# Turning the softmax blocks on VectorE and placing them by a DRAM copy, in a fused attention and gMLP block

## The chip, the cores and the metric

One Trainium2 chip, one of its cores. The metric is the device time of one execution in microseconds (us). All arrays are fp32; TensorE multiplies them as fp32r parts (a high part and a remainder, three products for one).

## What is computed

One layer of a hybrid decoder trunk over 1,024 tokens of width 1,024. With h the RMS-normalised input, one projection `h @ w_in` gives q, k, v, the gates and the inputs of the gMLP branch. The part that the change touches is the sliding-window attention: 16 query heads of width 64, 2 key/value heads, a window of 128 keys, a shared bias and one sink per head:

```
scores = q @ k.T * HEAD_DIM**-0.5 + bias        # a block of 128 queries against 256 keys, masked to the window
m      = max(max(scores), sink)
p      = exp(scores - m)
probs  = p / (sum(p) + exp(sink - m))
out    = probs @ v
y_a    = (out * silu(gate_a)) @ w_branch_a
merged = sigmoid(mg_a) * y_a + sigmoid(mg_b) * y_b
x      = x + rms_norm(merged @ w_out)
```

## The kernel before, in words

After a first stage (norm, v-branch, keys and values) come 24 column pairs n = 0 to 23 of the projection. A pair is made of seven products of twelve 128x512 matmuls each (a fast matrix scheme with seven products in the place of eight), so it has seven steps s = 0 to 6. Pairs 0 to 15 alternate: even n are "Q" pairs (query columns and their gate), odd n are "M" pairs (the two merge gates). Pairs 16 to 23 are "U" pairs (gMLP). After the pairs come three 1,024-cubed products in squares (branch A, branch B, output).

Attention is woven into the pairs. A head pair p (two heads, 0 to 7) has eight blocks of 128 queries. Its steps are counted by k: `attention_at(n, s)` gives p = (n - 1) // 2 and k = s for odd n, k = s + 7 for even n, so a head pair has fourteen steps, and attention ends inside pair 16. TensorE runs the first six matmuls of a product, then `attend(p, k)`, then the other six. In block order, for block k:

- step k: TensorE `scores` into the PSUM region `ps_s` (one buffer); VectorE merges the two key blocks by `copy_predicated` (line 2073), adds the bias, scales and takes the row's extreme (line 2076), into `neg_s`; ScalarE `exps` reads `neg_s` and writes `prob` (three buffers). GpSimd puts the sinks into `neg_s` at k = 0 (line 1788).
- step k+1: VectorE `reciprocal` (line 2057), ScalarE `norm` (line 1526).
- step k+3: TensorE `transpose_p` turns the two 128x128 blocks with the identity into `ps_p` in PSUM (line 997); VectorE makes the high part and the remainder from it into `pt_pack` (lines 2066 and 2067); GpSimd masks the copy for the previous keys into `pt_prev` (line 1796).
- step k+5: TensorE `values` (line 1017), two blocks to a group `g` in `ps_m`.
- at k = 7, 9, 11, 13: ScalarE moves a group's halves to `o_tmp` (lines 1541, 1542), VectorE adds them (lines 2086, 2087); at k = 8, 10, 12, 13 GpSimd multiplies by the gate (line 1806); SyncE stores to `ga_d` at k = 10 and 13.

Every engine walks the same list of pairs and steps in its own program order: at each step first `attend`, then `after(n, s)`, with waits on semaphores. So an engine that waits at one place holds up all behind it. In `after`, ScalarE copies TensorE's products out of PSUM and makes the high parts `w_hi` of the next weights, VectorE adds the products up (`c_11`, `c_22`, `c_21`, lines 2014, 2018, 2023), multiplies gates (line 2043) and, for U pairs, sums weights (lines 1998 to 2009) and runs the gMLP arithmetic (`u_mix` line 2100, `u_gate` line 2118), GpSimd makes the remainders `w_lo` (line 1751) and the weight sums of the pairs before 16. SyncE issues all DMAs: two 512 KB weight columns per pair into three `raw` buffers (line 499), the gates' stores, the bias tile of the next head pair at k = 8, and at pair 16, step 2, `bmat` and two mix tiles (lines 752 and 660) into `ub`, which lies over the keys, queries and bias of the attention.

## Time and the profile before

| | before |
|---|---|
| median of 3 runs | 908.63 us (907.77 to 910.6) |
| the profiled execution, its own time | 907.86 us |
| its span, first to last instruction | 906.1 us |
| TensorE busy | 898.7 us, 99% of the span |
| VectorE / ScalarE / GpSimd busy | 640.1 / 491.0 / 499.4 us |
| granted TensorE clock | 0.998 |
| DMA moved | 122.50 MB, 135 GB/s |

The span is what the trace covers; the execution's own time is 1.8 us more. TensorE overlaps successive matmuls, so that its busy time is best read as "no gaps", and the cost of a piece of its work from the distance between starts.

### The profile page before, as it was taken

The numbers are of one execution on the slowest core, as the hardware profiler recorded it, in microseconds if no ns is written. First come the engines' busy times: TensorE is split into PE (matmuls) and PEld (weight loads), VectorE is DVE, ScalarE is ACT, GpSimd is POOL, SyncE is SP. The second block draws the span as 40 slices with busy tenths as digits, with TensorE's granted clock in tenths as the row PEclk, the third lists the DMA queues.
The fourth block names the chain that finished last, engine by engine and source line by source line (L and its number), as shares of the span: only waits on it lengthen the run. The fifth ranks groups of instructions, "written<-read, shape, count | busy, mean of one in ns | idle before, by whom it ended". The sixth has DMA issues, their size and how long they took to land.

```text
span 906.1 us, 12649 instructions
## 1 busy us (share of the span) xinstructions
PE 898.7 (99%) x4332; PEld 754.0 (83%) x4332; DVE 640.1 (71%) x1135; ACT 491.0 (54%) x948; POOL 499.4 (55%) x395
## 2 busy tenths in 40 slices
PE   9999999999999999999999999999999999999997
PEld 7888888888888888888888888888888888888886
DVE  6766794655656564656565678688689878989968
ACT  6554355766756675757566664344444434534563
POOL 4565235777686868695868685445542252043236
PEclk9999999999999999999999999999999999999999
DMA  8889764422222253323222243533188550435004
GB/s 307 195 200 247 243 204 106 136 77 90 71 91 85 82 139 129 94 77 98 72 84 91 82 150 95 187 122 122 59 303 323 186 209 1 139 116 210 1 1 186
DMA packets 126591, 122.50 MB, mean 135 GB/s; under 512 B 23208, under 2 KB 95936, under 8 KB 126272
## 3 DMA queue, kind: packets, MB, share of 16 engines
q1 hardware_dynamic: 124288, 118.27, 41.2%
q10 hardware_dynamic: 2240, 3.43, 1.2%
q8 instruction: 35, 0.57, 0.3%
q14 instruction: 28, 0.23, 0.1%
HBM read 89.68 MB, written 35.15 MB: 138 GB/s over the span
## 4 chain that ended last, share of the span: by engine, by line
PE 98%; ACT 0%; DVE 0%; POOL 0%; issue 0%; DVEq 0%; POOLq 0%; ACTq 0%
PE acc L970 51%; PE acc L1150 11%; PE acc L823 9%; PE ps_m L1150 7%; PE ps_t L1150 7%; PE ps_t L987 3%; PE ps_m L1017 3%; PE acc L913 2%; PE ps_t L997 2%; PE ps_t L853 1%; PE ps_m L853 0%; PE acc L1042 0%; PE ps_t L839 0%; PE ps_t L855 0%; PE ps_m L855 0%
## 5 line engine op out<-in xcount | busy, mean ns | idle before, releaser
L970 PE MATMUL acc<-mv,w_hi 128*128 128x512 f32 x1344 | 353.1, 392 | 0.0
L970 PEld LDWEIGHTS acc<-mv,w_hi 128*128 128x128 f32 x1344 | 245.0, 188 | 45.0
L970 PE MATMUL acc<-mv,w_lo 128*128 128x512 f32 x672 | 181.1, 391 | 0.0
L970 PEld LDWEIGHTS acc<-mv,w_lo 128*128 128x128 f32 x672 | 126.2, 188 | 28.3
L1751 POOL TENSOR_TENSOR w_lo<-sums,w_hi 128x1024 fp32r<-128x1024 f32 x48 | 116.0, 2418 | 46.4 <-ACT w_hi L1316 38.4
L1751 POOL TENSOR_TENSOR w_lo<-raw,w_hi 128x1024 fp32r<-128x1024 f32 (+1 forms) x48 | 95.7, 1994 | 41.5 <-ACT w_hi L1309 35.9
L1150 PE MATMUL acc<-right,left 128*128 128x512 f32 x432 | 98.7, 389 | 0.0
L1150 PEld LDWEIGHTS acc<-right,left 128*128 128x128 f32 x432 | 81.0, 188 | 17.2 <-DVE left L2131 0.4
L1796 POOL TENSOR_SCALAR_AFFINE_SELECT pt_prev<-pt_pack 128x512 fp32r<-128x512 f32 x64 | 41.7, 652 | 85.7 <-DVE pt_pack L2067 85.7
L1518 ACT ACTIVATE prob<-neg_s,neg_max 128x129 f32<-128x129 f32 x128 | 50.6, 397 | 68.6 <-DVE neg_max L2076 68.5
L823 PE MATMUL acc<-mv 128*128 128x512 f32 x288 | 69.3, 394 | 0.6 <-ACT mv L1183 0.6
L1150 PE MATMUL ps_t<-right,left 128*128 128x512 f32 x288 | 67.2, 389 | 0.0
L1150 PE MATMUL ps_m<-right,left 128*128 128x512 f32 x288 | 67.2, 389 | 0.0
L1150 PEld LDWEIGHTS ps_m<-right,left 128*128 128x128 f32 x288 | 54.1, 188 | 11.2
L1150 PEld LDWEIGHTS ps_t<-right,left 128*128 128x128 f32 x288 | 54.1, 188 | 11.2
L823 PEld LDWEIGHTS acc<-mv 128*128 128x128 f32 x288 | 53.2, 188 | 12.1 <-ACT mv L1183 0.8
L2086 DVE TENSOR_TENSOR o_tmp<-ps_m,o_tmp 64x256 f32<-64x256 f32 x32 | 13.3, 417 | 63.6 <-ACT o_tmp L1542 62.9
L1526 ACT ACTIVATE prob<-prob,inv_den 128x128 f32<-128x128 f32 x128 | 43.9, 391 | 8.8 <-DVE inv_den L2057 8.8
L1368 ACT ACTIVATE c<-acc 128x512 f32<-128x512 f32 x24 | 14.4, 600 | 56.1 <-PE acc L970 46.2
L2066 DVE CAST pt_pack<-ps_t 128x256 fp32r<-128x256 f32 x64 | 26.8, 419 | 24.4 <-PE ps_t L997 24.1
L2076 DVE CUSTOM_DVE_ANT_0 neg_s<-ps_t,bias_t,sink_b 128x128 f32<-128x128 f32 x128 | 39.9, 349 | 2.0
L1757 POOL TENSOR_TENSOR left<-w_a,left 128x1024 fp32r<-128x1024 f32 x7 | 18.6, 2683 | 36.6 <-ACT left L1457 36.6
(282 smaller groups left out, 1680.8 us busy)
## 6 DMA issues: line engine op xcount, KB each, us to landing
raw<-in_w_in SPq DMA_DIRECT2D x56, 512.0 KB, 4.0
ht_d<-sums SPq DMA_DIRECT2D x8, 512.0 KB, 5.1
mix_d<-mix_b SPq DMA_DIRECT2D x8, 512.0 KB, 3.9
ga_d<-gate SPq DMA_DIRECT2D x16, 256.0 KB, 2.0
tb<-tb_d SPq DMA_DIRECT2D x4, 1024.0 KB, 5.2
ub<-mix_d SPq DMA_DIRECT2D x7, 512.0 KB, 3.5
gb_d<-ub SPq DMA_DIRECT2D x7, 512.0 KB, 2.6
x_both<-in_x SPq DMA_DIRECT2D x6, 512.0 KB, 6.3
```

What stands on the lines that cost most here:

```text
L823: ins = nc.tensor.matmul(acc[b][:, hf * HALF:(hf + 1) * HALF], left, right, start=(m < 2), stop=(m >= 46), skip_group_check=True)
L970: ins = nc.tensor.matmul(bank, (w_lo if y == 2 else w_hi)[:, left + k * P:left + (k + 1) * P], right[:, (OPW if y == 1 else 0) + k * HALF: ...
L987: ins = nc.tensor.matmul(ps_s[:, h * 256 + lo:(h + 1) * 256], q_st[h][:, blk * P:(blk + 1) * P], kbuf[:, kc + lo:kc + 256], start=a, stop= ...
L1017: ins = nc.tensor.matmul(o, v_st[:, v0:v0 + P], pt[blk % 2][:, y * 256:(y + 1) * 256].rearrange("p (h c) -> p h c", h=2), start=(kb == 0 a ...
L1150: ins = nc.tensor.matmul(bank, l[:, c:c + P], r[:, (OPW if y == 1 else 0) + k * HALF:(OPW if y == 1 else 0) + (k + 1) * HALF], start=(m == ...
L1518: ins = nc.scalar.activation(prob[blk % 3][:, h * SINK_W:(h + 1) * SINK_W], neg_w(blk, h), ACT.Exp, scale=-1.0, bias=neg_max[:, head(blk, ...
L1526: ins = nc.scalar.activation(w, w, ACT.Copy, scale=inv_den[:, head(blk, h)])
L1751: nc.gpsimd.tensor_tensor(w_lo[:, c], src, w_hi[:, c].bitcast(f32), ALU.subtract).then_inc(wlo_ok, 1)
L1757: ins = nc.gpsimd.tensor_tensor(left[f % 2][:, OPW:2 * OPW][:, c], left_src(f // 7, ORDER[f % 7])[:, c], left[f % 2][:, c].bitcast(f32), A ...
L1796: nc.gpsimd.affine_select(out=pt_prev[blk % 2][:, :].rearrange("p (y q) -> p y q", y=4), in_=pt_pack[blk % 2][:, :].rearrange("p (y q) -> ...
L2066: own.link(nc.vector.tensor_copy(pack[:, 0:256], ps_p))
L2076: ins = nc.vector.tensor_tensor_reduce(out=neg_w(k, h)[:, 0:P], in0=ps_s[:, h * 256 + P:(h + 1) * 256], in1=bias_t[:, bias:bias + P], scal ...
```

## The change

- TensorE's `transpose_p` is gone (128 transposes of 128x128), and so are `ps_p`, `neg_s` and the semaphores around them.
- VectorE writes the scaled scores straight into `prob`, which now has two buffers of two blocks each (a "double block"), and the sinks by a copy of two columns per block; ScalarE's `exps` works in place.
- After `norm`, VectorE turns each 128x128 block in place with `nc.vector.transpose`, which turns every 32x32 square where it stands. The squares are then brought to their places by DRAM: SyncE stores a double block (256 KB in rows of 512 bytes) to `prob_d` (`prob_away`, k = 2, 5, 8, 11), waits for the landing and reads it back with four DMAs of 64 KB in runs of 128 bytes into `turned_in`, one buffer (`prob_back`, k = 3, 6, 9, 12). `prob_back` also waits until VectorE has read the double block before out of `turned_in`.
- VectorE's high part and remainder are now made from `turned_in` in SBUF and no longer from PSUM.
- The eight blocks' scores go to steps 0, 1, 3, 4, 6, 7, 9, 10; high part and remainder to steps 5, 6, 8, 9, 11, 12, 14, 15; GpSimd's mask one step after, `values` two steps after these; the groups' ends to 9, 12, 15, 18 and the gate to 10, 13, 16, 19. So a head pair runs on for six steps under the next, and attention ends in pair 17.
- `o_tmp` has one buffer. The bias of the next head pair is loaded at k = 11. For pairs before 16 the weight loads move from steps 4 and 5 to steps 5 and 6. `load_k(1)` moves from pair 8 step 2 to step 4, the reload of `v_st` from pair 8 step 5 to pair 9 step 4. At pair 16, step 2, SyncE waits for `scores_used` of all 64 blocks in the place of `scores_ok`.
- Some semaphores and small tiles are shared with others to make room.

The core of the diff:

```diff
+BLOCK_AT = (0, 1, 3, 4, 6, 7, 9, 10)
+LAST_STEP = 20
+    prob_d = nc.dram_tensor("prob_d", [4 * HEAD_PAIRS, P, 4 * P], f32)
...
-                prob = [sb(f"prob{b}", [P, 2 * SINK_W], f32, s1) for b in range(3)]
-                o_tmp = [sb(f"o_tmp{b}", [P, 256], f32, s1) for b in range(2)]
+                prob = [sb(f"prob{b}", [P, 4 * SINK_W], f32, s1) for b in range(2)]
+                o_tmp = sb("o_tmp", [P, 256], f32, s1)
+                turned_in = sb("turned_in", [P, 512], f32, s1)
...
+        def attention_all(n, s):
+            k = 7 * (n - 1) + s
+            p = k // 14
+            last = [(p - 1, k % 14 + 14)] if 1 <= p <= HEAD_PAIRS and k % 14 + 14 < LAST_STEP else []
+            return last + ([(p, k % 14)] if 0 <= k and p < HEAD_PAIRS else [])
+        def blocks_at(k, lag):
+            return [i for i, t in enumerate(BLOCK_AT) if t + lag == k]
+        def low_at(k, lag):
+            return [i for i in range(8) if 3 * (i // 2) + i % 2 + lag == k]
...
+            def prob_away(j):
+                sp.wait_ge(turn_ok, 2 * j + 2)
+                sp.dma_start(prob_d[j, :, :].rearrange("p (c j) -> p c j", c=4),
+                             prob[j % 2][:, :].rearrange("p (c j) -> p c j", c=4)[:, :, 0:P]).then_inc(prob_out[j % 2], 16)
+            def prob_back(j):
+                sp.wait_ge(prob_out[j % 2], 16 * (j // 2 + 1))
+                if j:
+                    sp.wait_ge(ptl_ok, 2 * j)
+                for g in range(4):
+                    sp.dma_start(turned_in[32 * g:32 * (g + 1), :].rearrange("a (c q b) -> a c q b", c=4, q=4),
+                                 prob_d[j, :, :].rearrange("(q a) (c g b) -> g a c q b", q=4, c=4, g=4)[g]
+                                 ).then_inc(prob_in[j % 2], 16)
             def attend(p, k):
+                if k in (2, 5, 8, 11):
+                    prob_away(4 * p + k // 3)
+                if k in (3, 6, 9, 12):
+                    prob_back(4 * p + k // 3 - 1)
...
-                    if s == 4:
+                    if s == (5 if n < FIRST_U else 4):
                         load_pair(n + 2, 0)
-                    if s == 5:
+                    if s == (6 if n < FIRST_U else 5):
                         load_pair(n + 2, 1)
                     if n == FIRST_U and s == 2:
-                        sp.wait_ge(scores_ok, 8 * HEAD_PAIRS)
+                        sp.wait_ge(scores_used, 8 * HEAD_PAIRS)
                         sp.dma_start(bmat, bmat_d[:, :]).then_inc(bmat_in, 16)
...
-            def transpose_p(p, blk):
-                s = 8 * p + blk
-                pe.wait_ge(prob_ok, s + 1)
-                if s:
-                    pe.wait_ge(ptl_ok, s)
-                for h in range(2):
-                    ins = nc.tensor.transpose(ps_p[:, h * P:(h + 1) * P], prob[blk % 3][:, h * SINK_W:h * SINK_W + P],
-                                              ident[:, :])
-                ins.then_inc(pt_done, 1)
...
             def attend(p, k):
-                if 5 <= k < 13:
-                    values(p, k - 5)
-                if 3 <= k < 11:
-                    transpose_p(p, k - 3)
-                if k < 8:
-                    scores(p, k)
+                for blk in low_at(k, 7):
+                    values(p, blk)
+                for blk in blocks_at(k, 0):
+                    scores(p, blk)
...
+                for blk in low_at(k, 5):
+                    s = 8 * p + blk
+                    dve.wait_ge(prob_in[s // 2 % 2], 64 * (s // 4 + 1))
                     if s == 0:
                         dve.wait_ge(v_out, 16)
                     if s >= 2:
                         dve.wait_ge(values_ok, s - 1)
...
+                    turned = turned_in[:, s % 2 * 256:(s % 2 + 1) * 256]
+                    pack = pt_pack[s % 2]
+                    own.link(nc.vector.tensor_copy(pack[:, 0:256], turned))
+                    nc.vector.tensor_tensor(pack[:, 256:512], turned, pack[:, 0:256].bitcast(f32),
+                                            ALU.subtract).then_inc(ptl_ok, 1)
+                for blk in blocks_at(k, 1):
+                    s = 8 * p + blk
+                    dve.wait_ge(prob_ok, s + 1)
                     for h in range(2):
+                        w = prob_w(s, h, P)
+                        ins = nc.vector.transpose(w, w)
+                    ins.then_inc(turn_ok, 1)
```

## Rows read from the trace of the kernel before

**Rows 1.** The page's chain that ended last: shares of the span.

```profile
PE 98%; ACT 0%; DVE 0%; POOL 0%; issue 0%; DVEq 0%; POOLq 0%; ACTq 0%
```

**Rows 2.** Timeline of TensorE: start us, us, engine line op out<-in xcount.

```profile
402.84 0.28 PE L987 MATMUL ps_t<-k_hi,q_st 128*128 128x256 f32 x1
...
406.06 0.28 PE L987 MATMUL ps_t<-k_hi,q_st 128*128 128x256 f32 x1
...
409.29 0.38 PE L997 MATMUL ps_t<-ident,prob 128*128 128x128 f32 x2
...
412.73 0.38 PE L997 MATMUL ps_t<-ident,prob 128*128 128x128 f32 x2
...
438.05 0.40 PE L1017 MATMUL ps_m<-pt_pack,v_st 128*128 128x256 f32 x2
...
441.29 0.40 PE L1017 MATMUL ps_m<-pt_pack,v_st 128*128 128x256 f32 x2
...
538.39 1.98 PE L970 MATMUL acc<-mv,w_hi 128*128 128x512 f32 x8
...
541.11 1.98 PE L970 MATMUL acc<-mv,w_hi 128*128 128x512 f32 x8
```

**Rows 3.** Windows: one head pair, 399.8 to 447.4 us; busy (x) by engine, clock, DMA.

```profile
399.80:447.40 47.60, 47.60 (x248) 40.56 (x248) 27.49 (x84) 30.72 (x80) 35.21 (x30) 1.00 0.27 84
```

**Rows 4.** Single lines of VectorE: xcount: duration ns min/median/max, first and last start us.

```profile
L1905 DVE STREAM_TRANSPOSE sums<-x_both x4: 1234/1245/1246, 50.1 to 92.4; 128x1024 f32<-128x1024 f32 x4
L2076 DVE CUSTOM_DVE_ANT_0 neg_s<-ps_t,bias_t,sink_b x128: 341/349/355, 163.0 to 521.4; 128x128 f32<-128x128 f32 x128
L2492 DVE COPY gate<-gate x1: 229/229/229, 145.1 to 145.1; 128x128 f32<-128x128 f32 x1
L2067 DVE TENSOR_TENSOR pt_pack<-ps_t,pt_pack x64: 423/424/427, 172.1 to 532.8; 128x256 fp32r<-128x256 f32 x64
```

**Rows 5.** VectorE and GpSimd at the same moment: timelines around 542 us.

```profile
542.25 2.87 DVE L2118 SCALAR_TENSOR_TENSOR c<-ub,c 128x512 f32<-128x512 f32 x1
...
542.17 2.40 POOL L1751 TENSOR_TENSOR w_lo<-sums,w_hi 128x1024 fp32r<-128x1024 f32 x1
```

**Rows 6.** Timeline of VectorE around one block's softmax; idle before, releaser in brackets.

```profile
403.51 0.43 DVE L2073 COPY_PREDICATED ps_t<-before,ps_t 128x256 f32<-128x256 int32 x1 [0.48 <-PE ps_t L987]
...
404.26 0.35 DVE L2076 CUSTOM_DVE_ANT_0 neg_s<-ps_t,bias_t,sink_b 128x128 f32<-128x128 f32 x1
...
405.56 0.17 DVE L2057 RECIPROCAL inv_den<-row_sum 128x2 f32<-128x2 f32 x1 [0.95 <-ACT prob L1518]
```

**Rows 7.** Timeline of ScalarE: the norm of that block.

```profile
406.39 0.69 ACT L1526 ACTIVATE prob<-prob,inv_den 128x128 f32<-128x128 f32 x2
```

**Rows 8.** SyncE's issues of four DMAs in 128-byte runs, and their landing.

```profile
39.79 4.97 SPq L478 DMA_DIRECT2D x_both<-in_x  x4
...
DMA to landing us min/median/max: 3.4/5.3/11.5
```

**Rows 9.** The page's DMA issues: xcount, KB each, median us to landing.

```profile
raw<-in_w_in SPq DMA_DIRECT2D x56, 512.0 KB, 4.0
...
ga_d<-gate SPq DMA_DIRECT2D x16, 256.0 KB, 2.0
...
bias_t<-skew_d SPq DMA_DIRECT2D x8, 256.0 KB, 2.8
...
ub<-bmat_d SPq DMA_DIRECT2D x1, 512.0 KB, 5.0
```

**Rows 10.** Pair 16 and 17: SyncE, VectorE and ScalarE timelines.

```profile
524.54 0.44 SPq L752 DMA_DIRECT2D ub<-bmat_d  x1
...
533.73 1.27 DVE L2100 SCALAR_TENSOR_TENSOR ub<-ub,g_col 128x1024 f32<-128x1024 f32 x1
...
526.56 1.28 ACT L1419 ACT_TABLE_LOAD   x1
```

**Rows 11.** Timeline of TensorE in pair 16, old step 10.

```profile
533.28 0.40 PE L1017 MATMUL ps_m<-pt_pack,v_st 128*128 128x256 f32 x2
```

More of the change, by code:

```diff
@@ L36 @@
 ACT_H, ACT_WSH = (1, 3), 2
+BLOCK_AT = (0, 1, 3, 4, 6, 7, 9, 10)
+LAST_STEP = 20
+POOL_FRONT = 5
 Q_COL = 0
@@ L727, in _ @@
                 for s in range(7):
-                    at = attention_at(n, s)
-                    if at:
+                    for at in attention_all(n, s):
                         attend(*at)
@@ L1032, in product @@
                     product_mms(n, x, 0, 6)
-                    attend(*at)
+                    for one in at:
+                        attend(*one)
                     product_mms(n, x, 6, 12).then_inc(prod, 1)
@@ L2053, in attend @@
                     dve.wait_ge(bias_in, 16 * (p + 1))
-                if 1 <= k < 9:
-                    m2 = slice((k - 1) % 4 * 2, (k - 1) % 4 * 2 + 2)
-                    dve.wait_ge(exp_ok, 8 * p + k)
+                for blk in blocks_at(k, 1):
+                    m2 = slice(blk % 4 * 2, blk % 4 * 2 + 2)
+                    dve.wait_ge(exp_ok, 8 * p + blk + 1)
                     nc.vector.reciprocal(inv_den[:, m2], row_sum[:, m2]).then_inc(inv_ok, 1)
-                if 3 <= k < 11:
-                    s = 8 * p + k - 3
-                    dve.wait_ge(pt_done, s + 1)
+                for blk in blocks_at(k, 0):
+                    s = 8 * p + blk
+                    if s % 2 == 0 and s >= 4:
+                        dve.wait_ge(prob_out[s // 2 % 2], 16 * (s // 4))
+                    nc.vector.tensor_copy(prob[s // 2 % 2][:, :].rearrange("p (b h j) -> p b h j", b=2, h=2)[:, s % 2, :, P],
+                                          sink_b[:, 2 * p:2 * p + 2])
+                    dve.wait_ge(scores_ok, s + 1)
+                    if blk > 0:
+                        own.link(nc.vector.copy_predicated(blocks(ps_s)[:, :, 1, :], before_i, blocks(ps_s)[:, :, 0, :]))
+                    for h in range(2):
+                        bias = h * 256 + (0 if blk else P)
+                        ins = nc.vector.tensor_tensor_reduce(
+                            out=prob_w(s, h, P), in0=ps_s[:, h * 256 + P:(h + 1) * 256], in1=bias_t[:, bias:bias + P],
+                            scale=-HEAD_DIM ** -0.5, scalar=sink_b[:, 2 * p + h:2 * p + h + 1], op0=ALU.add, op1=ALU.min,
+                            accum_out=neg_max[:, head(blk, h)])
+                    ins.then_inc(scores_used, 1)
+                for blk in low_at(k, 5):
+                    s = 8 * p + blk
+                    dve.wait_ge(prob_in[s // 2 % 2], 64 * (s // 4 + 1))
                     if s == 0:
@@ L2064, in attend @@
                         dve.wait_ge(values_ok, s - 1)
-                    pack = pt_pack[(k - 3) % 2]
-                    own.link(nc.vector.tensor_copy(pack[:, 0:256], ps_p))
-                    nc.vector.tensor_tensor(pack[:, 256:512], ps_p, pack[:, 0:256].bitcast(f32), ALU.subtract).then_inc(ptl_ok, 1)
-                if k < 8:
-                    dve.wait_ge(scores_ok, 8 * p + k + 1)
-                    if 8 * p + k >= 2:
-                        dve.wait_ge(exp_ok, 8 * p + k - 1)
-                    if k > 0:
-                        own.link(nc.vector.copy_predicated(blocks(ps_s)[:, :, 1, :], before_i, blocks(ps_s)[:, :, 0, :]))
-                    for h in range(2):
-                        bias = h * 256 + (0 if k else P)
-                        ins = nc.vector.tensor_tensor_reduce(
-                            out=neg_w(k, h)[:, 0:P], in0=ps_s[:, h * 256 + P:(h + 1) * 256], in1=bias_t[:, bias:bias + P],
-                            scale=-HEAD_DIM ** -0.5, scalar=sink_b[:, 2 * p + h:2 * p + h + 1], op0=ALU.add, op1=ALU.min,
-                            accum_out=neg_max[:, head(k, h)])
-                    ins.then_inc(scores_used, 1)
-                if k >= 7 and k % 2:
-                    g = (k - 7) // 2
+                    turned = turned_in[:, s % 2 * 256:(s % 2 + 1) * 256]
[3 more added lines that the diff above has]
+                                            ALU.subtract).then_inc(ptl_ok, 1)
+                for blk in blocks_at(k, 1):
+                    s = 8 * p + blk
+                    dve.wait_ge(prob_ok, s + 1)
+                    for h in range(2):
+                        w = prob_w(s, h, P)
+                        ins = nc.vector.transpose(w, w)
+                    ins.then_inc(turn_ok, 1)
+                if k in (9, 12, 15, 18):
+                    g = (k - 9) // 3
                     gg = 4 * p + g
```

130 lines of the change are left out of this document (54 added, 76 removed).

## Prediction, written before the changed kernel ran

> **What bounds the kernel now.** The page's chain that ended last comes first: 98% of the span is TensorE [rows 1], so work taken from TensorE shortens the kernel unless another engine makes it wait. How much an instruction costs it is not in its own duration, since matmuls overlap; it is in the distance from start to start, so the timeline of TensorE comes second [rows 2]. A step without attention takes 2.72 us (538.39 to 541.11); with scores alone 3.22; with transposes and scores 3.44; with values alone 3.24 (438.05 to 441.29). The pairs run without a gap, so the clock of the step is TensorE's alone. Third come the windows of one head pair: 47.6 us at full clock, with VectorE busy 27.5, ScalarE 30.7 and GpSimd 35.2 [rows 3]. These three have room as a sum. What can still hold TensorE is a single value that comes late.
>
> **Part 1, the transposes go.** 3.44 less 3.22 is 0.22 us for the two transposes of a block; another pair of steps in the same timeline gives 0.21. 64 blocks at 0.21 are 13.4 us. That scores, values and products share the steps in another way changes little: scores cost 0.50 (3.22 less 2.72) and values 0.52 (3.24 less 2.72), a little of it for breaking into the product, and I take 0.2 us off for one more step per head pair that both share. A head pair falls from 47.6 to about 45.9 us, a step to 3.28 on average. Sum for TensorE: 13.6 us less.
>
> **Part 2, VectorE's new work.** No row shows a transpose of 128x128 alone. The nearest is 1,024 columns in 1.245 us, so an eighth, 0.16 us, is the floor, and the ceiling is the 0.35 us of another operation on 128 columns [rows 4]. I take 0.27, between the two, since short operations carry a fixed part: 16 in a head pair are 4.3 us (2.5 to 5.6). The Trainium skill has a number for this, in VectorE: DVE Perf Modes, "The three transpose paths": 311 ns for a bf16 block of 128x128; by it the 16 would take 5.0 us. The sink copies cost up to 0.23 each, as a copy of 128 columns does [rows 4]; at 0.1 for two columns they add 0.8 us per head pair. The high part is now read from SBUF, at most 0.42 as before. So 27.5 us become 32.6 (31 to 35) of 45.9: room for 13 us of waits. On the path of TensorE this costs nothing, as long as VectorE has each score block done before the next scores are due.
>
> **Part 3, the trip through DRAM.** I write T(k) for TensorE's scores or values of step k, steps 3.28 us apart. In the old trace scores start at 402.84; VectorE ends with them about 404.5, the reciprocal comes at 405.56 [rows 6], the norm ends at 407.1 [rows 7], 4.2 us after the scores' start. So the second block of a double block, with scores at T(1), is turned at about T(2) + 1.5. The store: 256 KB took 2.0 us for the gates, 2.8 for the bias tile with shorter rows [rows 9]; landed by T(3) + 1.0. The read must also wait until VectorE has split the double block before, at step 3, behind that step's scores: about T(3) + 2.5. Four such DMAs of twice the runs took 4.97 us to issue [rows 8], so here I take half, 2.5 (up to 5.0 if the number of runs did not matter); the last is issued 1.9 us in and lands 3.4 to 5.3 us later [rows 8]. The data are there at T(3) + 7.8 to 9.7, which is T(5) + 1.2 to 3.1. VectorE stands ready for them at T(5) - 0.6, so it waits 1.8 to 3.7 us at this place (steps 8 and 11 of the new list; steps 5 and 14 hang on the store alone and wait less). The cover for this wait: values come at T(7), and splitting (0.84) and GpSimd's mask (0.64) are done 2 to 4 us before. Queued behind the wait are the turning of the next block and, in the next step, its score block, which must be through 1.7 us before T(7): splitting and turning end at T(5) + 2.7 to 4.6, the limit is T(5) + 4.9. So it is hidden, with 0.3 to 2.2 us to spare. ScalarE is not held, since the reciprocal comes ahead of the wait. Price in the sum: 0.
>
> SyncE's other duties: the first weight column of a pair is issued a step later and behind the four reads. Issued near T(12) + 3.5 and 4.0 us on its way [rows 9], it lands about T(14) + 1; ScalarE wants it some 2.3 us after T(14). Nothing, with a microsecond to spare. Keys and `v_st` at the change of the key head have two or more steps for 4 to 7 us. Nothing.
>
> **Part 4, pair 16.** This is the one place where I see a new stall. `bmat` and the mix tiles were issued at 524.54, 9 us before VectorE's `u_mix` at 533.73 [rows 10], which is TensorE's old step 10 at 533.28 plus 0.4 [rows 11]. Now SyncE waits until VectorE has read the last scores, at new step 10, about T(10) + 1.7, and 5.0 us of landing follow [rows 9], with the mix tile just behind: T(10) + 6.9. `u_mix` stands in the same step, so VectorE is held about 5 us and ends it at T(10) + 8.2. Behind it wait the split of block 4 (done T(10) + 9.2) and then the mask, while values want it at T(13) = T(10) + 9.8: 0 to 2.5 us of stall, the latter if a GpSimd operation of 2.4 us is in front. The last double block is turned late as well, goes out and back in about 9 us, and its values at step 16 may wait another 0 to 2.5 us. ScalarE also has to go from the exponential to Gelu and back while blocks 6 and 7 are still due; a table load is 1.28 us [rows 10], two more of them. I put 2.5 us for pair 16 and 17 together, 0 to 7.
>
> **Sum.** The profiled execution took 907.86 us, span 906.1 and 1.8 around it. 907.86 - 13.4 - 0.2 + 2.5 = 896.8. The median of the runs shown, 908.63, stands 0.8 above that execution, so I predict 897.5.
>
> **Rivals.** (a) The forecast: the gain of TensorE stays, less some microseconds at pair 16: 894.2 to 901. Chance 0.66.
>
> (b) VectorE fills up through GpSimd. The two operations that split a block now work from SBUF to SBUF, where before one side was PSUM and their time was steady, 423 to 427 ns [rows 4]. VectorE's operation at 542.25 on SBUF tiles took 2.87 us beside a GpSimd operation of 2.40 us that began just before, and ended 0.6 us after it [rows 5]: it had stood behind it. GpSimd is busy 35.2 of 45.9 us, so an operation may meet it three times in four and wait 1.2 us on average, 0.9 in all; 16 in a head pair would be 14.7 us where 13.3 are free. That is 1.4 us over, 8 times: 11 us, and with it 908. Against it: GpSimd's mask waits for the split, so it is often idle just then; by half the contention all fits. The waits of part 3 use the same room, though. Chance 0.17, between 901 and 908, most likely about 904. The Trainium skill says the same of the shared path (GPSIMD Engine Reference, its table of interfaces): contention comes with VectorE instructions that have two SBUF inputs or use both ports; the trace agrees in the row just named.
>
> (c) The reads in 128-byte runs are slow, and the kernel ends slower. The place is `prob_back` at steps 6 and 9 of each head pair, 16 times in all; there it decides from a landing of 5.6 us for the last piece on (0.3 above the median row), and the gain is gone at about 6.5 us, since 16 stalls of 0.9 us are 14 us. The largest landing in the row is 11.5 us, under other traffic [rows 8]. At 8.0 us it is 16 times 2.4, or 38 us: 935. For it: the median lies right under the limit, and the issue could take 5.0 us and not 2.5. Against it: a read here is half as large, and the DMA engines are busy 0.27 of the time in the pairs [rows 3]. Chance 0.14. A page of the Trainium skill speaks against the change here: VectorE: DVE Perf Modes, "The three transpose paths", warns that a plain copy which transposes by strides is 19 times slower than the hardware's transposing DMA. Here the strides move whole runs of 32 numbers, and no row shows the transposing DMA.
>
> (d) The change does not do what it says: TensorE's transposes were free and the time stays at 908. Only the missing gaps in [rows 2] speak on it, and they speak against it. Chance 0.03.
>
> **Numbers.** What this kernel's measurement can tell from no change is about 0.3%, 2.7 us: 905.9 to 911.4. Faster: all of (a), most of (b), a little of (c): 0.81. Same: the end of (b), (d), a sliver of (c): 0.08. Slower: 0.11. The range that leaves 2 in 10 out runs from 894.2 (no stall at all) to 905.5, up into (b); the forecast's own is 894.2 to 901.
>
> **What would show it.** Steps with values and scores 3.71 us apart and steps with scores alone 3.22, no transpose group on TensorE, a head pair of 45.9 us: part 1. A transpose line of 0.2 to 0.35 us, 128 times: part 2. VectorE's idle time ahead of the split ended by the DMA into `turned_in`, 1.8 to 3.7 us each, and no idle time of TensorE at scores or values: part 3. VectorE idle for about 5 us ahead of `u_mix` in pair 16, and TensorE idle by 2.5 us in pairs 16 and 17: part 4. For (b) the split's two lines would stretch to means over 1 us; for (c) the landing of the last read would be over 5.6 us and TensorE would stand at scores, released by VectorE. I am wrong if another place, such as a weight column that lands late, holds TensorE every pair.

## The result and the profile after

| | before | after |
|---|---|---|
| median (lowest to highest) | 907.92 us (907.77 to 910.6) | 948.16 us (945.63 to 954.06) |
| ratio, 95% interval | | 1.0445 (1.0421 to 1.0469) |
| the profiled execution, its own time / span | 907.86 / 906.1 us | 954.06 / 952.3 us |

The changed kernel is 4.4% slower; 897.5 us had been predicted. The profiled execution is the slowest of the five, 5.9 us above their median. 3.6 us of its distance to the kernel before lie ahead of the attention: the first pair's products start at 115.6 us and not at 112.0, behind a wait of 2.30 us for VectorE. So the waits below are somewhat larger than those of a median execution. The page of the changed kernel shows what answers to [rows 1], the chain that ended last, and then its groups and DMA issues.

```profile
PE 44%; DVE 24%; DMA 12%; ACT 7%; issue 7%; SPq 6%; POOL 1%; ACTq 0%; DVEq 0%; POOLq 0%
...
L1003 PE MATMUL acc<-mv,w_hi 128*128 128x512 f32 x1344 | 359.7, 399 | 27.5 <-ACT c L1389 18.2
...
L2089 DVE CAST pt_pack<-turned_in 128x256 fp32r<-128x256 f32 x64 | 38.0, 593 | 26.3 <-DMA turned_in<-prob_d 26.3
L2097 DVE STREAM_TRANSPOSE prob<-prob 128x128 f32<-128x128 f32 x128 | 32.3, 291 | 22.7 <-ACT prob L1544 21.0
...
raw<-in_w_in SPq DMA_DIRECT2D x56, 512.0 KB, 5.0
prob_d<-prob SPq DMA_DIRECT2D x32, 256.0 KB, 2.7
turned_in<-prob_d SPq DMA_DIRECT2D x128, 64.0 KB, 2.6
```

TensorE held 98% of the chain before and holds 44% now; it waits, and its longest group waits for a ScalarE copy, `c` at line 1389. That copy empties the accumulator for the next product. The window of [rows 3] after the change (busy by engine, clock, DMA share, GB/s):

```profile
399.80:447.40 47.60, 44.64 (x215) 37.08 (x214) 33.23 (x92) 28.05 (x73) 32.76 (x26) 0.96 0.43 109
```

TensorE has gaps of 3 us in it and a lower clock. VectorE is busy 33.2 of the 47.6 us; it is not full. A head pair, from its first scores to those of the next, lasts 51.7 us on average (48.0 to 54.4), where 45.9 had been worked out; steps that nothing holds are as predicted, 3.23 us with scores alone and 3.70 with scores and values. Two places per head pair are the longest: step 11 to 13 takes 7.8 to 10.3 us (5.96 without a wait, a step with values and one with nothing) and step 2 to 3 takes 4.0 to 6.3 (3.24). Here is the first, from behind to front. TensorE's timeline, the last column being the idle time before and what ended it:

```profile
407.56 0.28 PE L1020 MATMUL ps_t<-k_hi,q_st 128*128 128x256 f32 x1
...
411.72 1.09 PE L1003 MATMUL acc<-mv,w_lo 128*128 128x512 f32 x4
415.28 3.63 PE L1003 MATMUL acc<-mv,w_hi 128*128 128x512 f32 x8 [2.47 <-ACT c L1389]
```

ScalarE at that moment:

```profile
413.77 0.40 ACT L1536 ACTIVATE prob<-prob,neg_max 128x129 f32<-128x129 f32 x1 [0.94 <-DVE neg_max L2075]
...
414.56 0.57 ACT L1389 ACTIVATE c<-acc 128x512 f32<-128x512 f32 x1
```

And VectorE, on which ScalarE waited:

```profile
402.92 2.17 DVE L2089 CAST pt_pack<-turned_in 128x256 fp32r<-128x256 f32 x1 [2.06 <-DMA turned_in<-prob_d]
...
407.20 1.04 DVE L2089 CAST pt_pack<-turned_in 128x256 fp32r<-128x256 f32 x1
408.27 1.40 DVE L2090 TENSOR_TENSOR pt_pack<-turned_in,pt_pack 128x256 fp32r<-128x256 f32 x1
...
412.02 0.61 DVE L2068 COPY prob<-sink_b 128x2 f32<-128x2 f32 x1
412.64 0.43 DVE L2072 COPY_PREDICATED ps_t<-before,ps_t 128x256 f32<-128x256 int32 x1
```

The scores of 407.56 are touched by VectorE only at 412.64, 5 us later. Ahead of them stand a wait of 2.06 us for the block that was read back, splits (high part and remainder) that take 2.17, 1.04 and 1.40 us where some last 0.3 and 0.4, other adds, and the sink copy. ScalarE's exponential can't start, and the copy that frees the accumulator stands behind it in ScalarE's program order. TensorE stops for 2.47 us. Then it pays again: its eight matmuls take 3.63 us and not 1.98 [rows 2], 1.65 us more. A window row of the stretch after the gap gives the granted clock, 0.53, which is the 1.2 GHz level; the stretch from 420 us on is at 1.00:

```profile
415.20:418.80 3.60, 3.52 (x9) 2.87 (x10) 2.52 (x8) 2.80 (x6) 1.23 (x2) 0.53 0.08 26
420.00:424.00 4.00, 4.00 (x21) 3.36 (x20) 2.07 (x3) 2.13 (x3) 3.66 (x4) 1.00 0.54 106
```

Over the whole profiled execution the granted clock was 0.985, and 0.998 before. As an estimate (0.013 of 952.3 us), up to 12 us of this execution's loss are not waits but the slower pace that followed them.

SyncE's queue at the end of the same head pair:

```profile
419.91 2.60 SPq L646 DMA_DIRECT2D turned_in<-prob_d  x4
422.61 0.57 SPq L513 DMA_DIRECT2D raw<-in_w_in  x1
423.23 0.58 SPq L660 DMA_DIRECT2D ga_d<-gate  x1
423.90 0.38 SPq L513 DMA_DIRECT2D raw<-in_w_in  x1
```

The pair's two weight columns leave within 1.3 us of each other, the first one behind four reads and 1.5 us after the values of step 13, at 421.07. In the trace of before both left from 440.37 on, 0.9 us ahead of the values of step 12 [rows 2]:

```profile
440.37 2.96 SPq L499 DMA_DIRECT2D raw<-in_w_in  x2
```

In the changed kernel, ScalarE's `w_hi` at 427.49 stood idle 0.58 us for it.

### The profile page after: what moved, and what is told of

Its sections match the earlier page's. It is cut to its first block, busy times and chain, and to the rows that moved or that the text cites. A ratio compares the mean times of both kernels' runs of the same rounds, so it can differ in the third digit from the quotient of the medians.

```text
span 952.3 us, 12590 instructions
## 1 busy us (share of the span) xinstructions
PE 906.4 (95%) x4204; PEld 748.6 (79%) x4204; DVE 718.2 (75%) x1327; ACT 491.7 (52%) x950; POOL 497.0 (52%) x387
## 2 busy tenths in 40 slices
DMA packets 211072, 139.29 MB, mean 146 GB/s; under 512 B 91304, under 2 KB 180416, under 8 KB 210752
## 4 chain that ended last, share of the span: by engine, by line
PE 44%; DVE 24%; DMA 12%; ACT 7%; issue 7%; SPq 6%; POOL 1%; ACTq 0%; DVEq 0%; POOLq 0%
PE acc L1003 10%; PE acc L1171 10%; PE ps_m L1171 7%; PE ps_t L1171 7%; PE acc L856 6%; DMA raw<-in_w_in 6%; SPq L646 3%; DVE prob L2068 3%; DMA turned_in<-prob_d 3%; DVE pt_pack L2089 2%; DVE prob L2075 2%; DMA prob_d<-prob 2%; DVE ps_t L2072 2%; DVE pt_pack L2090 2%; ACT prob L1536 2%
## 5 line engine op out<-in xcount | busy, mean ns | idle before, releaser
L1003 PE MATMUL acc<-mv,w_hi 128*128 128x512 f32 x1344 | 359.7, 399 | 27.5 <-ACT c L1389 18.2
L1003 PEld LDWEIGHTS acc<-mv,w_hi 128*128 128x128 f32 x1344 | 249.2, 192 | 80.9 <-issue 33.9
L1536 ACT ACTIVATE prob<-prob,neg_max 128x129 f32<-128x129 f32 x128 | 50.6, 396 | 112.1 <-DVE neg_max L2075 112.1
L2089 DVE CAST pt_pack<-turned_in 128x256 fp32r<-128x256 f32 x64 | 38.0, 593 | 26.3 <-DMA turned_in<-prob_d 26.3
L2097 DVE STREAM_TRANSPOSE prob<-prob 128x128 f32<-128x128 f32 x128 | 32.3, 291 | 22.7 <-ACT prob L1544 21.0
L2075 DVE CUSTOM_DVE_ANT_0 prob<-ps_t,bias_t,sink_b 128x128 f32<-128x128 f32 x128 | 39.9, 349 | 2.0
L1020 PE MATMUL ps_t<-k_hi,q_st 128*128 128x256 f32 (+1 forms) x128 | 34.3, 290 | 3.7 <-DVE neg_max L2075 2.0
```

The source lines that it names most:

```text
L1003: ins = nc.tensor.matmul(bank, (w_lo if y == 2 else w_hi)[:, left + k * P:left + (k + 1) * P], right[:, (OPW if y == 1 else 0) + k * HALF: ...
L1020: ins = nc.tensor.matmul(ps_s[:, h * 256 + lo:(h + 1) * 256], q_st[h][:, blk * P:(blk + 1) * P], kbuf[:, kc + lo:kc + 256], start=a, stop= ...
L1536: ins = nc.scalar.activation(w, w, ACT.Exp, scale=-1.0, bias=neg_max[:, head(blk, h)], accum_out=row_sum[:, head(blk, h)])
L2075: ins = nc.vector.tensor_tensor_reduce(out=prob_w(s, h, P), in0=ps_s[:, h * 256 + P:(h + 1) * 256], in1=bias_t[:, bias:bias + P], scale=-H ...
L2089: own.link(nc.vector.tensor_copy(pack[:, 0:256], turned))
L2097: ins = nc.vector.transpose(w, w)
```

## The experiments

Each was timed in turns with the kernel before on the same chip, in five sets on four chips; the medians of the kernel before lie between 907.9 and 908.6 us, so differences of 2 or 3 us between experiments of different sets are not certain. Ratios are to the kernel before, with 95% intervals. "The trip" is the way of the turned blocks through DRAM.

**1. Without the trip.** VectorE splits each block from `prob`; the squares stay where they stand, so the outputs are of unplaced squares.

```diff
-                if k in (2, 5, 8, 11):
-                    prob_away(4 * p + k // 3)
-                if k in (3, 6, 9, 12):
-                    prob_back(4 * p + k // 3 - 1)
...
-                    turned = turned_in[:, s % 2 * 256:(s % 2 + 1) * 256]
+                    turned = prob[s // 2 % 2][:, :].rearrange("p (b h j) -> p b h j", b=2, h=2)[:, s % 2, :, 0:P]
```

> The changed kernel without the trip through DRAM: no store to prob_d, no reads, and VectorE splits the turned squares where they lie in prob (so the squares are not brought to their places). All else as changed, the tile turned_in stays allocated. If the trip is what holds TensorE, the stalls go: 895 to 900 us. If VectorE's operations that share a path with GpSimd are the cause, nearly nothing changes: 935 to 950 us. If the new places of the steps and of the weight loads are the cause, also 935 to 950 us. A value between says how the 54 us above the floor of 894 are divided.

Measured: 924.89 us, 1.0182 (1.0167 to 1.0197). The trip costs 23 us, in what it makes TensorE wait and in the lower clock after the waits: without it the granted clock was 0.997 to 1.0. Without the trip the kernel is still 17 us slower than before, with a head pair of 48.9 us. So there are at least two causes.

**2. Turned into PSUM.** As 1, but VectorE writes the turned squares to the PSUM region that TensorE's transposes had used and splits from there (squares unplaced).

```diff
+                        ins = nc.vector.transpose(ps_p[:, h * P:(h + 1) * P], prob_w(s, h, P))
...
+                    own.link(nc.vector.tensor_copy(pack[:, 0:256], ps_p))
```

> As the kernel without the trip (the squares are not brought to their places), but VectorE turns a block at the step of the split and writes it to PSUM, so that the two split operations read PSUM as in the kernel before; the same count of VectorE operations. If sharing the path with GpSimd matters, this is faster than the kernel without the trip, by up to 20 us if that one stays above 930 us. If it does not matter, the two agree within 3 us. Nothing to gain if the kernel without the trip is already at 895 us.

Measured: 914.24 us, 1.0067 (1.0052 to 1.0082). The splits' means are 425 and 424 ns, as in [rows 4], where the kernel of 1 had 596 and 564 (and single ones of up to 2.5 us). The step is worth 10.7 us in all, not for the splits alone: VectorE also turns a block later, at the step of its split, and the sink copies got shorter (453 ns on average, 692 in 1). They still stood out (groups of VectorE, 200 to 500 us, of this kernel; count, then busy us and mean ns):

```profile
L2088 DVE CAST pt_pack<-ps_t 128x256 fp32r<-128x256 f32 x52 | 22.1, 425 | 1.8
L2089 DVE TENSOR_TENSOR pt_pack<-ps_t,pt_pack 128x256 fp32r<-128x256 f32 x52 | 22.1, 424 | 1.8
L2063 DVE COPY prob<-sink_b 128x2 f32<-128x2 f32 x50 | 20.8, 416 | 0.0
```

**3. TensorE turns, on the new list of steps.** The transposes are back on TensorE, at lag 5; scores, values and groups keep their new steps.

```diff
+                for blk in low_at(k, 5):
+                    transpose_p(p, blk)
```

> The spread alone: the changed kernel's steps, buffers and weight loads, but TensorE turns the blocks with the identity into PSUM, at the step of the split, as in the kernel before; no turning on VectorE and no trip. If the spread is harmless, TensorE's 13.4 us are back and the time is that of the kernel before: 906 to 911 us. If the spread or the later weight loads cost by themselves, it is above 915 us.

Measured: 925.62 us, 1.0194 (1.0179 to 1.0209), head pairs of 48.5 us where TensorE alone would need 47.6. Though nothing is turned by VectorE and nothing leaves the core, the new list with the sink copies loses 17.6 us. So VectorE's transposes can't be the whole of it. Only 5.8 us of the 17.6 are lost by the first scores of the last head pair (500.7 us from the start, 494.9 before). The rest lies behind, in pairs 16 and 17, where TensorE waits 1.56 us and then 5.16 us (at 549.25) for a split of VectorE's and runs at a granted clock of 0.78 over the 12 us from 548.7. How much of the 17.6 the sink copies make was not tried here.

**4. Read in place.** The blocks come back into the buffer that they left, so that no read waits for the split of the double block before.

```diff
-                if j:
-                    sp.wait_ge(ptl_ok, 2 * j)
...
-                    sp.dma_start(turned_in[32 * g:32 * (g + 1), :] ...
+                    sp.dma_start(prob[j % 2][32 * g:32 * (g + 1), 4:516] ...
```

> The changed kernel, complete, with one thing different: the reads from DRAM land in the prob buffer that was stored, and no longer in the single tile turned_in, so that SyncE need not wait for the split of the double block before. If the gate on the single buffer is what makes the data late (my step with the read at T(3) + 2.5 in the place of T(3) + 1.0), the reads come 1.5 us earlier at steps 6 and 9 and much of the loss goes: 905 to 920 us. If the trip's length or VectorE's load is the cause, it stays at 935 to 948 us.

Measured: 946.91 us, 1.0417 (1.0399 to 1.0434), against 948.16: nothing within the spread. The single `turned_in` is not the cause.

**5. The sinks by ScalarE**, on the kernel of 2.

```diff
-                    nc.vector.tensor_copy(prob[...][:, s % 2, :, P], sink_b[:, 2 * p:2 * p + 2])
+                nc.scalar.activation(prob[...][:, s % 2, :, P], sink_b[:, 2 * p:2 * p + 2], ACT.Copy).then_inc(sink_ok, 1)
```

> As the kernel without the trip that turns into PSUM (914.2 us; the squares are not brought to their places), but the 64 sink copies of two columns are made by ScalarE and not by VectorE, where they take 453 ns each on average and up to 1.5 us. If their sharing a path with GpSimd holds VectorE ahead of the scores, the head pairs lose up to 0.3 us for each: 905 to 911 us. If the remaining stalls of 1.4 us per head pair have another cause, 913 to 916 us.

Measured: 903.48 us, 0.9937 (0.9914 to 0.996), 10.8 us less for moving 64 copies of two columns. ScalarE does one in 192 ns. The cost of one on VectorE shows in the trace of the changed kernel. First VectorE, then GpSimd:

```profile
446.63 1.47 DVE L2068 COPY prob<-sink_b 128x2 f32<-128x2 f32 x1
```

```profile
445.66 2.41 POOL L1768 TENSOR_TENSOR w_lo<-sums,w_hi 128x1024 fp32r<-128x1024 f32 x1 [3.60 <-ACT w_hi L1337]
```

Both end at 448.1. The line's durations run from 124 to 1498 ns, and in the trace of the changed kernel each of the 39 copies that took over 0.3 us ended within 0.03 us of the end of a GpSimd operation that had begun before it; no other copy lay wholly inside one. So a copy of two columns waits out GpSimd's operation when it meets one. The splits do the same: all 15 high parts over 0.5 us ended 0.15 us after a GpSimd operation, all 8 such remainders 0.28 us after one. The Trainium skill describes this (SBUF — State Buffer, "SBUF: two separate sides"): the port pair that VectorE and GpSimd share is locked for a whole instruction, and by the box under that section a plain fp32 copy inside SBUF is one that takes it. The trace agrees with the two rows above.

**6. The mix of pair 16 at step 5** instead of step 3, on the kernel of 2.

```diff
-                    if kind(n) == "U" and n < PAIRS - 1:
+                    if kind(n) == "U" and FIRST_U < n < PAIRS - 1:
                         u_mix(n)
...
+                if s == 5 and n == FIRST_U:
+                    u_mix(n)
+                    u_mul(n, 0)
```

> As the kernel without the trip that turns into PSUM (914.2 us; the squares are not brought to their places), but in pair 16 VectorE does u_mix and the first u_mul at step 5 and not at steps 3 and 4, so that it no longer stands for bmat and the mix tile with the split of blocks 4 and 5 behind it. The gap between TensorE's values at new steps 11 and 13 of the last head pair is 11.87 us there and 6.3 in the head pairs before. If the wait for bmat makes it, the gap falls to about 6.3 us and the time to about 908.5 us. If not, it stays.

Measured: 911.15 us, 1.0025 (1.001 to 1.0041), 3.1 us less, where some 5.7 had been expected: step 11 to 13 fell to 8.3 us and not to 6.3.

**7. Loads back at steps 4 and 5**, behind the same step's trip, on the changed kernel.

```diff
-                    if s == (5 if n < FIRST_U else 4):
+                    if s == 4:
```

> The changed kernel, complete, with the weight loads of the pairs before 16 back at steps 4 and 5 (they had been moved to 5 and 6). If the late weight columns are a part of the loss (ScalarE stood 11.2 us for them in all, up to 5.5 at a time), this is 10 to 20 us faster than 948. If the reads' own way is the cause, it is the same or slower, since the reads now stand behind the loads.

Measured: 945.15 us, 1.0385 (1.0354 to 1.0416), 3 us less, where 10 to 20 had been expected if late columns were a part of the loss. Moving the loads alone, still behind the trip's transfers, gives little.

**8. One plain read** of 256 KB in place of four in 128-byte runs (squares unplaced), on the changed kernel.

```diff
-                for g in range(4):
-                    sp.dma_start(turned_in[32 * g:32 * (g + 1), :] ...
+                sp.dma_start(turned_in[:, :], prob_d[j, :, :]).then_inc(prob_in[j % 2], 64)
```

> The changed kernel, but a double block is read back by one DMA of 256 KB in rows of 2 KB, as it lies in prob_d (the squares are not brought to their places), in the place of four DMAs in 128-byte runs. SyncE issues for 0.4 us and not for 2.6. If issuing the four DMAs and their small runs are what makes the trip cost 23 us, the time falls to 926 to 932 us, near the kernel without the trip (924.9). If it is the trip's fixed length (store, landing, read, landing), it stays at 940 us or more.

Measured: 934.84 us, 1.0284 (1.0251 to 1.0318). This lies between the two expectations: 13 of the trip's 23 us go with the four issues and their small pieces. VectorE's wait for the block read back fell from 26.3 to 13.0 us.

**9. Sinks by ScalarE and the late mix, trip and all.** The edits of 5 and 6 on the changed kernel.

> The changed kernel whole, with two things moved: the sink columns are written by ScalarE (10.7 us less on the kernel that turned in PSUM) and pair 16's mix waits until step 5 (3.1 us less there). Theory A, VectorE's own work sets these steps even with the trip in place: both add up, 934 to 936 us. Theory B, with the trip in place VectorE is waiting anyway, so what it saves only lengthens its wait for the returned blocks: the sinks give under 4 us and the time stays at 941 to 945.

Measured: 927.63 us, 1.0199 (1.0176 to 1.0223), 20.5 us less where 14 had been expected. So VectorE's own work sets these steps with the trip too. A reading that fits, and that no run here isolates: a copy of 0.6 us ahead of a score block costs more once the wait for the trip has used up the slack.

**10. Three softmax buffers, three more steps.** Read in place as in 4; split, mask and values move to lags 8, 9 and 10, groups' ends by three steps.

```diff
-                for blk in low_at(k, 5):
+                for blk in low_at(k, 8):
```

> The changed kernel whole, with three softmax buffers instead of two, the returned blocks read back into the buffer that they left, and the split, the mask and the value products three steps later. The trip is as long and issues as much, but has three more steps. Theory A, the trip costs because it comes back too late for its step: most of its 23 us return, 926 to 932 us. Theory B, it costs through the time that it takes of SyncE and of the DMA engines, so that weight columns come late: at most the 10 us of its length return, 938 us or more.

Measured: 952.34 us, 1.0482 (1.0444 to 1.0519). VectorE no longer waits for a block from DRAM at all (26.3 us in the changed kernel), and nothing is gained. I had believed that the trip came back too late; that alone was not it. The waits stood elsewhere now (engine, line, waited for: us, times, longest):

```profile
PE acc L1000 <- ACT ev L1372: 18.8, 13, 2.8
PE acc L1000 <- ACT c L1386: 10.9, 9, 1.8
```

```profile
DVE prob L2094 <- ACT prob L1541: 35.6, 25, 1.9
DVE o_tmp L2101 <- ACT o_tmp L1557: 31.9, 21, 2.7
```

**11. Three buffers, sinks by ScalarE, late mix.**

> Three buffers with three more steps, and the sinks by ScalarE and the late mix of pair 16 too. If lateness, the sink copies and the mix are separate causes, they add: 14 us under the kernel with three buffers alone, about 914 to 918. If they cover one another (a stall in the same place, paid once), it is less than 8 us under it.

Measured: 924.63 us, 1.0179 (1.0134 to 1.0225): 27.7 us under 10, twice what had been expected, and 3 under 9. The same sinks again, larger still.

**12. The high part by ScalarE**, on 11.

```diff
-                    own.link(nc.vector.tensor_copy(pack[:, 0:256], turned))
+                    nc.scalar.activation(pt_pack[s % 2][:, 0:256], prob[...][...], ACT.Copy).then_inc(hi_ok, 1)
```

> As the one before, and the high part of the split is made by ScalarE: VectorE loses 8 copies of some 0.59 us for each head pair, 38 us in all, and ScalarE gains 8 of some 0.4. Theory A, VectorE is what is late in the steps with both a score and a split: 5 to 8 us less, 907 to 912, at the time of the kernel before. Theory B, ScalarE is the later one (its evictions of the value products hold TensorE): no less, or up to 5 us more.

Measured: 960.82 us, 1.0574 (1.0524 to 1.0624), 36 us more: both expectations missed. Two things show. TensorE's waits for ScalarE's `ev` copy grew from 10.1 to 24.7 us, since the new ScalarE operation stands in its queue ahead of the copies; that this order is the reason is read from the program, not isolated. And what VectorE gave up came back in part, since its remainder was stretched (its group, 200 to 500 us; in the kernel of 11 its mean was 865 ns):

```profile
L2102 DVE TENSOR_TENSOR pt_pack<-prob,pt_pack 128x256 fp32r<-128x256 f32 x46 | 62.4, 1357 | 46.8 <-issue 35.6 <-ACT pt_pack L1565 11.3
```

**13. Loads first**, on 9: each step's weight load is issued ahead of that step's softmax transfers, at steps 4 and 5.

```diff
                 for s in range(7):
+                    if s == 4 and n < FIRST_U:
+                        load_pair(n + 2, 0)
+                    if s == 5 and n < FIRST_U:
+                        load_pair(n + 2, 1)
                     for at in attention_all(n, s):
                         attend(*at)
```

> Two softmax buffers, the sinks by ScalarE and the late mix of pair 16 (927.6 us), and each step's weight load is issued by SyncE ahead of the softmax transfers of that step, at steps 4 and 5 as in the kernel before. Theory A, late weight columns make ScalarE late, and through it TensorE: 915 to 922 us. Theory B, the reads come back later by as much as the loads come sooner, and VectorE waits for them: within 3 us of 927.6.

Measured: 920.86 us, 1.0136 (1.0107 to 1.0164), 6.8 us less. The edit changes two things, the order and, as in 7, the step; 7 had given 3 us for the step alone.

**14. The same on 11**, with three buffers.

> The same order of the loads with three softmax buffers and three more steps of the trip (924.6 us without it). Under theory A this is the version in which nothing of the trip is on the path: the reads may come late and the loads come early, so 902 to 912 us. Under a theory C, what the trip costs is the traffic itself (4 MB out and 4 MB back, all in small pieces) beside the engines, the order of the issues changes nothing: 921 to 926.

Measured: 918.92 us, 1.0115 (1.0087 to 1.0142), 5.7 us less than 11, but only 2 under 13, which their spreads (917.4 to 921.9 and 919.4 to 923.6) can't tell apart. It missed the 902 to 912 of theory A. (The traffic named under theory C is 8.4 MB out and 8.4 MB back, not 4: 32 double blocks of 256 KB, and the pages have 139.29 MB against 122.50.)

**15. VectorE adds a group's halves one step later**, on 14, so that it no longer meets ScalarE's copy of the same step at the head of its queue. GpSimd's product with the gate and the store follow by one step too.

```diff
-                if k in (12, 15, 18, 21):
-                    g = (k - 12) // 3
+                if k in (13, 16, 19, 22):
+                    g = (k - 13) // 3
```

> As the one before, and VectorE adds ScalarE's half of a group of values one step later, so that it doesn't wait for ScalarE at the head of its queue (25 us of such waits in the kernel with three buffers and the sinks by ScalarE). If these waits pass on a late ScalarE to the next scores: 3 to 8 us less than the one before. If they only stand where VectorE has time: no change.

Measured: 913.36 us, 1.0053 (1.0035 to 1.0071), 5.6 us less. Three of the seven distances between head pairs are now 45.88 us, as long as TensorE alone needs; two are near 50, at the reloads in the middle.

**16. One plain read, on 11** (squares unplaced).

> The kernel with three buffers, the sinks by ScalarE and the late mix (924.6 us), with the returned pair of blocks read by one transfer of whole rows, that leaves the squares unplaced: the trip has its length and its bytes, but one issue of some 0.6 us in place of four of 2.6 together, and no 128-byte pieces. Theory A (SyncE's queue, late loads): 905 to 913 us. Theory C (bytes): 921 or more.

Measured: 914.67 us, 1.0065 (1.004 to 1.009), 10 us less than 11 and just above what theory A allows. The bytes are the same, so these 10 us belong to the four issues or to the small pieces that go with them.

**17. All loads first**, on 15: the reloads of keys and values in the middle, and the loads from pair 16 on, stand ahead of the trip too.

```diff
+                    if n == FIRST_U - 8 and s == 4:
+                        sp.wait_ge(scores_ok, 8 * HEAD_PAIRS // 2)
+                        load_k(1)
+                    if n == FIRST_U - 7 and s == 6:
+                        sp.wait_ge(values_ok, 8 * HEAD_PAIRS // 2)
+                        sp.dma_start(v_st[:, :].bitcast(i32), v_d[:, :]).then_inc(v_in, 16)
                     for at in attention_all(n, s):
                         attend(*at)
```

> The kernel with three softmax buffers, the sinks by ScalarE, the adds one step later and the weight loads first (913.4 us), and now the two reloads in the middle (the second key head, the second half of the values) stand ahead of the softmax transfers of their step too, and the loads of pairs 16 and 17 as well. In its profile TensorE waits 3.3 and 1.4 us for these two reloads, at a lower granted clock afterwards, and 3.9 us in pair 17. If SyncE's order is what is left: 906 to 909 us, the time of the kernel before. If VectorE in pairs 16 and 17 is: 910 to 912.

Measured: 904.53 us (903.48 to 908.62), 0.9956 (0.9942 to 0.997): 8.8 us less than 15, a little more than expected, and 4.1 under the kernel before. This is the whole computation, with blocks turned by VectorE and placed through DRAM, and it beats both kernels. Its window of one head pair and all of TensorE's waits:

```profile
399.80:447.40 47.60, 47.60 (x241) 40.39 (x241) 36.27 (x106) 31.38 (x89) 37.19 (x31) 1.00 0.54 141
```

```profile
PE acc L1001 <- ACT ev L1373: 4.3, 1, 4.3
PE ps_m L1038 <- POOL pt_prev L1808: 1.9, 3, 0.8
PE acc L1059 <- DVE before L2439: 1.1, 1, 1.1
PE acc L854 <- DVE mv L1933: 0.3, 1, 0.3
PE ps_t L1018 <- DVE neg_max L2078: 0.2, 1, 0.2
```

TensorE has no gap in the window, though VectorE is busier than in the changed kernel (36.3 against 33.2 us) and its high part is stretched to a mean of 716 ns. What is left lies late: the waits for `pt_prev` at 534 to 545 us, and the wait of 4.3 us at 582. There ScalarE had stood 9.3 us for a weight column that SyncE issued at 571.5, right behind two loads of `g_a`; the eight matmuls after it took 3.75 us.

## Why the prediction was wrong, point by point

**Part 1, TensorE's work: right.** 3.23 and 3.70 us had been given as 3.22 and 3.71. The head pair of 45.9 us shows as soon as nothing holds it: 45.88 in six of seven in 17.

**Part 2, VectorE's new work: "On the path of TensorE this costs nothing" failed, and one term was mis-sized.** Without the trip the kernel took 924.9 us, 30 over the 895 of TensorE's work alone, so Part 2 and the new list were not free. A transpose took 0.291 us (0.27 taken, inside 0.16 to 0.35), 0.3 us more per head pair. The sink copy was taken at 0.1 us and bounded at 0.23, from one copy of 128 columns [rows 4]; it took 0.581 on average (37.2 us in 64) and up to 1.5. It was counted as load, and VectorE had room for load. But it stands directly ahead of the score block, on the way scores, exponential, copy of the accumulator, next product. Moving it to ScalarE gave 10.8 us without the trip and, after taking off the 3.1 of the mix, about 17 with it.

**Rival (b): the mechanism was real, in a milder form and in more places.** The split's lines had means of 593 and 565 ns, not over 1 us, and every long one ended with a GpSimd operation. Turning into PSUM made them steady (424 to 427 ns) and gave 10.7 us, in part through shorter sink copies. I had applied it to the split only, and judged it by whether VectorE would be full. It never was.

**Part 3, "Price in the sum: 0": the step that failed most.** The trip's price was 23 us (948.2 with it, 924.9 without) and not 0. Its transfers were no slower than forecast: the store landed in 2.7 us (2.0 to 2.8 taken), the reads were issued in 2.6 (2.5) and landed in 2.6 (3.4 to 5.3). VectorE's 15 waits for it were 1.8 us on average and 4.4 at most, near the 1.8 to 3.7 of the forecast. Two conclusions from it were wrong. First, the limit was set at VectorE's next score block, which must be through for the next scores. The tighter limit is ScalarE's: its exponential of the same step waits for VectorE, and behind that stands the copy that frees the accumulator for a product that TensorE starts one step later. "ScalarE is not held, since the reciprocal comes ahead of the wait" looked at one of the two things that ScalarE needs from VectorE. Second, the weight columns had "nothing, with a microsecond to spare". The first was issued 1.7 us before T(14), at 422.61 against 424.3, and not 3.1 as I had it, and ScalarE could start on it at T(14) + 3.2 and not at + 2.3; the microsecond to spare was gone. Loads first, with the step they were moved back by, gave 6.8 and 5.7 us, all reloads first 8.8 more.

**Rival (c) did not happen.** It was to decide from a landing of 5.6 us on; the median was 2.6 and the longest of 128 was 5.4. It was to be cured by slack, and 10 gave the trip three steps of slack for nothing. The four issues cost time, but through SyncE's queue or the engines' share in the small pieces, and not by coming back late.

**Part 4, pair 16: the place was right, the size was not.** 2.5 us had been taken, of 0 to 7. Step 11 to 13 took 11.76 us there, where 5.96 would do; SyncE issued `bmat` at 572.17 and VectorE's `u_mix` began at 577.59, after 3.32 us of waiting. About 6 us were lost there, and 3.1 us come back by moving the mix. The whole stretch lost more: from the first scores of the last head pair to the end of the pairs' products the changed kernel took 191.1 us, and the kernel before 176.9. In 17 it is still 187.7, so what 17 has left over TensorE's work lies for the most part there.

**The sum.** The changed kernel lost about 53 us to waits, over the 895 or so (908.6 less 13.6) that TensorE's work alone asks; up to 12 of them are the lower clock after the waits, an estimate from the profiled execution. By the order in which they were taken away: sinks and mix 20.5, loads first 6.8, three buffers 2 (within the spread), adds later 5.6, reloads first 8.8; 9.6 are left in 17. The shares depend on that order, as 5, 9 and 11 show for the sinks (10.8, about 17, about 25).

**What stays open.** Why the single read of 8 and 16 saves 13 and 10 us: the four issues in SyncE's queue or the 128-byte pieces themselves; four issues of whole rows would tell and were not tried. Whether the three buffers are needed for 15 and 17: the later adds and the reloads were not tried with two. What the new list of steps costs by itself: 3 still has the sink copies on VectorE and the wait of pair 16.

## What to carry to other kernels

When work is woven into another engine's steps, follow each engine's program order past the instruction that waits: what counts is the first thing behind it that frees a buffer of the bound engine, here a ScalarE copy two places behind the exponential. Price small operations by the worst they can meet on a shared path, when they stand ahead of such a chain. And place the loads that are needed on time ahead of transfers that themselves wait, before giving up a change as too slow: the same idea went from 948 to 904.5 us, most of it by who does the sink copies and by the order of work and loads, with a third softmax buffer.

## What the runs showed of the hardware

- A VectorE copy of two columns inside SBUF took 0.12 to 1.5 us; all 39 of the 64 that took over 0.3 us ended with a GpSimd operation. ScalarE did the same in 0.19.
- High part and remainder of a 128x256 block read from SBUF took 0.27 to 2.4 and 0.42 to 2.5 us; read from PSUM (2) both took 0.42 to 0.43 every time.
- A gap of 2.47 us on TensorE was followed by eight matmuls at a granted clock of 0.53, the 1.2 GHz level, which cost another 1.65 us. In pair 16 a gap of 2.90 us was followed by eight matmuls in 2.08 us, at nearly their usual pace; a gap does not always lower the clock. Of the 15 gaps over 1 us in the changed kernel's trace, 8 were followed by the lower level, the shortest of them 1.82 us.
- The high part made by ScalarE relieved VectorE by less than its own time: the remainder, which stayed on VectorE, was stretched from 865 to 1357 ns on average, where the high part had taken VectorE 627.
